# Three of four rows of each key chunk to GpSimd, and five key chunks moved from the state stage into the even projection

## The chip, the core and the metric

The kernel runs on one core of a Trainium2 chip. Its engines work side by side and meet only at semaphores: TensorE (PE) multiplies matrices, VectorE (DVE), ScalarE (ACT) and GpSimd (POOL) work on vectors, SyncE (SP) issues transfers. The metric is the device time of one execution in microseconds; lower is better. What follows reads one profiled execution of the kernel before, and the order of instructions of both.

## The reference

The reference is one step of a two-layer decoder for a prompt of 512 tokens and eight samples with one new token each. Layer 0 joins differential attention and a gated linear attention behind one input projection; layer 1 is a recurrent block; each ends with an MLP. What matters here is the attention of the eight samples to 4096 cached positions:

```python
k_past = cache_k[li, page_table].reshape(Bd, P, DA_HEADS, 2 * DA_DH)
v_past = cache_v[li, page_table].reshape(Bd, P, DA_HEADS, DA_VD)
...
def logits(qh, kp, kn):
    lp = jnp.einsum('bqhd,bkhd->bhqk', qh, kp).astype(jnp.float32) * scale + bias_p
...
a = diff_probs(logits(q1, kp1, kn1), logits(q2, kp2, kn2), lam)
out = (jnp.einsum('bhqk,bkhd->bqhd', a[..., :P], v_past.astype(jnp.float32))
       + jnp.einsum('bhqk,bkhd->bqhd', a[..., P:], v_new.astype(jnp.float32)))
```

Per cached position and head there are two dot products of length 64 (q1 with k1, q2 with k2), so a row of 512 numbers (4 heads x 2 x 64) gives eight scores.

## The kernel before

The trunk holds all 520 tokens in SBUF as 8 tiles of 128 x 520. Each weight matrix comes in chunks of 1024 x 256 into RAW; ScalarE rounds a chunk to W_hi (line 793), VectorE computes W_lo = RAW - W_hi (`split_lo`, line 1260), and TensorE forms three products per tile (line 1850). W_hi and W_lo have two slots each. The even projection has 13 chunks (the last one with one tile); behind it come 16 attention units of the prompt (four heads times four query blocks), then eight steps of the gated linear attention (the state stage), then the output projection, the MLP and layer 1.

The cache passes beside this. Keys and values of the eight samples are 64 chunks each, eight per sample; a chunk is 128 partitions x 4 rows x 512 numbers in float32, 1.05 MB, fetched by an indirect transfer that GpSimd issues (line 731) into a ring of six buffers, KV. GpSimd issues the next transfer into a buffer when both users of it are done.

A key chunk n is worked as follows. VectorE multiplies rows 0 and 1 with the sample's query, which it reads from PSUM (line 1351, `k_first`), into the first half of PROD and reduces over 64 (line 1353). GpSimd multiplies rows 2 and 3 with a copy of the query in SBUF, QB (line 664, `pool_product`), into the second half of PROD, and VectorE reduces that in line 1339 (`k_second`). Each half of PROD has one buffer: `pool_product(n)` waits for `prod1_used >= n`, that is for the reduction of product n-1. In `k_chunks` the order on VectorE is: reduction of product n-1, multiplication n, its reduction; behind the last chunk of a sample the product is reduced at once, and the sample's row maxima follow (lines 1370 to 1374).

When VectorE works key chunks is written out by hand. In the projection it is `IN_STEPS` chunks behind the split of each weight chunk from the third on, so the split for chunk c+1 stands ahead of the key chunks of iteration c. `PRE_STEPS` are two groups of three behind the projection; behind the second comes line 1529, IDENTL, with which the units start. `UNIT_STEPS` is one per unit, `GLA_STEPS` up to three per state step. The same tables set the order of transfers (`load_order`: in a unit value, key, value; in a state step pairs of key and value), the slots in which the softmax of a sample is done (`steps_by_slot`), and where GpSimd takes the inverse roots for the norms (`power`, lines 688 and 692: behind certain value chunks, or ahead of certain key chunks), on which VectorE waits in line 1525.

The value chunks are multiplied by TensorE (line 2043), two in a unit and three in a state step, behind their transfers and GpSimd's copy of the weights into PM (line 677).

## Time and profile before

| | us |
|---|---|
| median of 3 runs | 1561.07 |
| lowest and highest | 1558.76 to 1563.27 |
| profiled execution, its own time | 1562.6 |
| its span | 1560.8 |
| TensorE busy | 1409.8 (90%) |
| VectorE busy | 886.9 (57%) |
| ScalarE busy | 513.3 (33%) |
| GpSimd busy | 325.6 (21%), all but 7 of it ahead of 520 us |

Read it by stages: the projection runs to 189 us, the units start at about 222, the state stage at about 368, and its end with the output projection's start lies between 513 and 540. A busy share is the mean of a stretch; a wait in the middle of one engine's queue holds everything behind it. "Idle before" in a row is the time for which the engine stood still ahead of that group, and the arrow names what ended it.

### The profile page before, as it was taken

The numbers are of one execution on the slowest core, as the hardware profiler recorded it, in microseconds if no ns is written. First come the engines' busy times: TensorE is split into PE (matmuls) and PEld (weight loads), VectorE is DVE, ScalarE is ACT, GpSimd is POOL, SyncE is SP. The second block draws the span as 40 slices with busy tenths as digits, with TensorE's granted clock in tenths as the row PEclk, the third lists the DMA queues.
The fourth block names the chain that finished last, engine by engine and source line by source line (L and its number), as shares of the span: only waits on it lengthen the run. The fifth ranks groups of instructions, "written<-read, shape, count | busy, mean of one in ns | idle before, by whom it ended". The sixth has DMA issues, their size and how long they took to land.

```text
span 1560.8 us, 26108 instructions
## 1 busy us (share of the span) xinstructions
PE 1409.8 (90%) x11324; PEld 1269.0 (81%) x11324; DVE 886.9 (57%) x1166; ACT 513.3 (33%) x829; POOL 325.6 (21%) x263
## 2 busy tenths in 40 slices
PE   4999957798777698999999999999989999999995
PEld 3999833345334398999999999899989999999995
DVE  3398978767797526534344343788456344343534
ACT  3322254433332334212222123476343222221213
POOL 1175768766776100000000000000000000000000
PEclk8999979876677799999999999899999999999998
DMA  8477699988889721332232232222213223232221
GB/s 316 135 273 243 232 323 387 375 332 318 334 319 347 280 84 44 108 100 90 84 107 83 84 107 76 87 67 72 83 56 107 82 88 103 82 104 86 82 82 55
DMA packets 127896, 250.37 MB, mean 160 GB/s; under 512 B 5267, under 2 KB 108455, under 8 KB 111136
## 3 DMA queue, kind: packets, MB, share of 16 engines
q0 software_dynamic: 18432, 134.23, 22.5%
q1 hardware_dynamic: 104064, 106.05, 21.2%
q10 hardware_dynamic: 5288, 8.45, 1.7%
q8 instruction: 89, 1.46, 0.4%
q14 instruction: 23, 0.19, 0.0%
HBM read 241.04 MB, written 7.73 MB: 159 GB/s over the span
## 4 chain that ended last, share of the span: by engine, by line
PE 78%; DVE 9%; ACT 4%; POOL 4%; issue 2%; DMA 2%; ACTq 0%; DVEq 0%; POOLq 0%
PE PS L1850 66%; PE PS L2043 3%; POOL PROD L664 2%; DVE SC L1339 1%; DMA KV<-in_cache_v,CIDX 1%; PE PS L2127 1%; PE PS L1834 1%; PE PS L2030 1%; POOL KV L731 1%; PE PS L1842 1%; DVE ST L1571 1%; PE PS L2085 1%; DMA XSIN<-in_x_sample 1%; DVE ACC L1751 1%; PE PS L1944 1%
## 5 line engine op out<-in xcount | busy, mean ns | idle before, releaser
L1850 PE MATMUL PS<-H_hi,W_hi 128*128 128x260 f32 x1936 | 399.4, 288 | 21.2 <-DVE H_lo L1314 9.7
L1850 PE MATMUL PS<-H_lo,W_hi 128*128 128x260 f32 x1936 | 394.8, 286 | 0.0
L1850 PE MATMUL PS<-H_hi,W_lo 128*128 128x260 f32 x1936 | 394.6, 286 | 0.0
L1850 PEld LDWEIGHTS PS<-H_hi,W_hi 128*128 128x128 f32 x1936 | 304.5, 192 | 27.0 <-issue 19.2
L1850 PEld LDWEIGHTS PS<-H_lo,W_hi 128*128 128x128 f32 x1936 | 303.6, 192 | 0.0
L1850 PEld LDWEIGHTS PS<-H_hi,W_lo 128*128 128x128 f32 x1936 | 303.6, 192 | 0.0
L1260 DVE TENSOR_TENSOR W_lo<-RAW,W_hi 128x2048 fp32r<-128x2048 f32 x91 | 210.5, 2313 | 134.7 <-ACT W_hi L793 134.6
L793 ACT ACTIVATE W_hi<-RAW 128x2048 fp32r<-128x2048 f32 x91 | 173.7, 1909 | 277.2 <-PE PS L1850 276.6
L1850 PE MATMUL PS<-U_hi,W_lo 128*128 128x260 f32 x1024 | 206.4, 283 | 0.0
L1850 PE MATMUL PS<-U_lo,W_hi 128*128 128x260 f32 x1024 | 206.0, 283 | 0.0
L1850 PE MATMUL PS<-U_hi,W_hi 128*128 128x260 f32 x1024 | 206.0, 282 | 0.0
L664 POOL TENSOR_TENSOR PROD<-KV,QB 128x1024 f32<-128x1024 f32 x64 | 152.0, 2375 | 122.1 <-DVE SC L1339 93.4
L1850 PEld LDWEIGHTS PS<-U_hi,W_hi 128*128 128x128 f32 x1024 | 157.9, 188 | 0.0
L1850 PEld LDWEIGHTS PS<-U_hi,W_lo 128*128 128x128 f32 x1024 | 157.9, 188 | 0.0
L1850 PEld LDWEIGHTS PS<-U_lo,W_hi 128*128 128x128 f32 x1024 | 157.4, 188 | 0.0
L1703 DVE TENSOR_TENSOR ACC<-ACC,PS 128x520 f32<-128x520 f32 x64 | 44.5, 696 | 197.8 <-PE PS L1850 197.8
L737 POOL MEMSET ACC<- 128x4160 f32 x2 | 7.1, 3572 | 649.3 <-DVE TMP L1285 649.3
L1100 ACT ACTIVATE UF<-SQ 128x520 f32<-128x520 f32 x64 | 40.8, 638 | 253.3 <-DVE SQ L1670 253.3
L1670 DVE SCALAR_TENSOR_TENSOR SQ<-PS,RS 128x520 f32<-128x520 f32 x64 | 44.6, 699 | 109.2 <-PE PS L1850 109.2
L2043 PE MATMUL PS<-KV,PM 128*32 128x512 f32 x512 | 88.5, 780 | 19.3 <-DMA KV<-in_cache_v,CIDX 9.8
L1351 DVE TENSOR_TENSOR PROD<-KV,PS 128x1024 f32<-128x1024 f32 x64 | 77.4, 1210 | 9.0 <-ACT QB L849 8.9
L731 POOL DMA_INDIRECT KV<-in_cache_k,CIDX x64 | 70.4, 1101 | 53.2 <-DVE TMP L1285 23.1
(300 smaller groups left out, 1423.4 us busy)
## 6 DMA issues: line engine op xcount, KB each, us to landing
RAW<-in_w_up SPq DMA_DIRECT2D x32, 1024.0 KB
RAW<-in_w_down SPq DMA_DIRECT2D x32, 1024.0 KB
RAW<-in_w_in_even SPq DMA_DIRECT2D x13, 1024.0 KB
RAW<-in_w_in_odd SPq DMA_DIRECT2D x8, 1024.0 KB
RAW<-in_w_out_odd SPq DMA_DIRECT2D x5, 1024.0 KB
RAW<-in_w_out_even SPq DMA_DIRECT2D x4, 1024.0 KB
x_saved<-X ACTq DMA_DIRECT2D x1, 2080.0 KB, 9.9
X<-x_saved SPq DMA_DIRECT2D x1, 2080.0 KB, 7.7
```

Of the source, the lines that this page charges most:

```text
L664: nc.gpsimd.tensor_tensor(PROD[:, 1], KV[i % RING][:, 2:4, :], QB[:, None, b % 2, :].to_broadcast([P, 2, 512]), ALU.mult).then_inc(prod1_r ...
L731: po.indirect_dma_start(KV[i % RING].rearrange("p n f -> p (n f)"), None, cache[kind], bass.IndirectOffsetOnAxis(ap=CIDX[:, n:n + 1], axis ...
L793: A(W_hi[:, ch.slot], RAW[:, ch.slot], ACT.Copy).then_inc(w_hi_ready, 1)
L1100: A(UF[:, i], RL[:, i], ACT.Square).then_inc(uf_ready, 1)
L1260: V.tensor_tensor(W_lo[:, ch.slot], RAW[:, ch.slot], W_hi[:, ch.slot].bitcast(F32), ALU.subtract).then_inc(w_lo_ready, 1)
L1339: V.tensor_reduce(k_scores(n, 1), PROD[:, 1].rearrange("p n (j d) -> p n j d", d=DH), AX.X, ALU.add).then_inc(prod1_used, 1)
L1351: V.tensor_tensor(PROD[:, 0], KV[i % RING][:, 0:2, :], PS[:, None, 6 + b % 2, :].to_broadcast([P, 2, 512]), ALU.mult).then_inc(k_used, 1)
L1571: V.scalar_tensor_tensor(ST[:, hp, state(tb, n + 1)], ST[:, hp, state(tb, n)], DECC[:, hp, 8 * tb + n:8 * tb + n + 1], update(n, slice(0, ...
L1670: V.scalar_tensor_tensor(pair(RL[:, i]), tile_banks(ch, i), 0.0, pair(RS[:, 1]), ALU.max, ALU.mult).then_inc(banks_free[ch.par[i]], 1)
L1703: V.tensor_tensor(pair(ACC[:, m]), pair(ACC[:, m]), banks(ch.par[i]), ALU.add).then_inc(banks_free[ch.par[i]], 1)
L1850: t = MM_(PS[:, 2 * bank + j, 0:HALF], w[:, ch.slot, k, cols], x[:, k, half], start=k == 0 and n == 0, stop=k == KT - 1 and n == 2)
L2043: t = MM_(PS[32 * pos:32 * pos + 32, 4, :], PM[:, part % 2, at:at + 32], KV[i % RING][:, pos, :], start=n % 32 == 0, stop=n % 32 == 31)
```

## The change

GpSimd's product covers rows 1 to 3 of each key chunk instead of 2 and 3, and VectorE multiplies row 0 alone. PROD keeps its size of 8 KB per partition. Of VectorE's two reductions the first covers one row, the second three. The projection's iterations take 2, 2, 3, 2, 3, 2, 3, 2, 3, 2, 3 key chunks, 27 in all instead of 22. The state steps take 3, 3, 3, 2, 2, 2, 0, 0, which is 15 instead of 20. The units and the two groups ahead of them keep their numbers. The places of the roots on GpSimd follow.

```diff
-    PROD = sb("PROD", [P, 2, 2, 512], F32, r_t)
+    PROD = sb("PROD", [P, 4, 512], F32, r_t)
...
-    IN_STEPS, PRE_STEPS = 2, (3, 3)
+    IN_STEPS, PRE_STEPS = [2, 2, 3, 2, 3, 2, 3, 2, 3, 2, 3], (3, 3)
     UNIT_STEPS = [1] * 16
-    GLA_STEPS = [3, 3, 3, 3, 3, 3, 2, 0]
+    GLA_STEPS = [3, 3, 3, 2, 2, 2, 0, 0]
...
-            nc.gpsimd.tensor_tensor(PROD[:, 1], KV[i % RING][:, 2:4, :], QB[:, None, b % 2, :].to_broadcast([P, 2, 512]),
+            nc.gpsimd.tensor_tensor(PROD[:, 1:4], KV[i % RING][:, 1:4, :], QB[:, None, b % 2, :].to_broadcast([P, 3, 512]),
                                     ALU.mult).then_inc(prod1_ready, 1)
...
-        POWERS_BEFORE_K = {K_IN_UNITS: (14, 15), **{K_IN_UNITS + 3 * u + 1: (15 + u,) for u in range(1, 7)}}
-        POWER_BEHIND_V = {**{2 * u + 1: u - 1 for u in range(1, 15)}, 53: 22, 57: 23}
+        POWERS_BEFORE_K = {K_IN_UNITS: (14, 15), **{K_IN_UNITS + sum(GLA_STEPS[:u]) + 1: (15 + u,) for u in range(1, 6)}}
+        POWER_BEHIND_V = {**{2 * u + 1: u - 1 for u in range(1, 15)}, 50: 21, 53: 22, 57: 23}
...
-            pos = 4 * (n % 8) + 2 * half
-            return SC[n // 8 % SLOTS][:, :, pos:pos + 2].rearrange("p j n -> p n j")
+            pos = 4 * (n % 8)
+            rows = slice(pos + 1, pos + 4) if half else slice(pos, pos + 1)
+            return SC[n // 8 % SLOTS][:, :, rows].rearrange("p j n -> p n j")
...
-            V.tensor_reduce(k_scores(n, 1), PROD[:, 1].rearrange("p n (j d) -> p n j d", d=DH), AX.X, ALU.add).then_inc(prod1_used, 1)
+            V.tensor_reduce(k_scores(n, 1), PROD[:, 1:4].rearrange("p n (j d) -> p n j d", d=DH), AX.X, ALU.add).then_inc(prod1_used, 1)
...
-            V.tensor_tensor(PROD[:, 0], KV[i % RING][:, 0:2, :], PS[:, None, 6 + b % 2, :].to_broadcast([P, 2, 512]), ALU.mult).then_inc(k_used, 1)
+            V.tensor_tensor(PROD[:, 0:1], KV[i % RING][:, 0:1, :], PS[:, None, 6 + b % 2, :], ALU.mult).then_inc(k_used, 1)
             ve.wait_ge(k_used, n + 1)
-            link(V.tensor_reduce(k_scores(n, 0), PROD[:, 0].rearrange("p n (j d) -> p n j d", d=DH), AX.X, ALU.add))
+            link(V.tensor_reduce(k_scores(n, 0), PROD[:, 0:1].rearrange("p n (j d) -> p n j d", d=DH), AX.X, ALU.add))
...
-                k_chunks(IN_STEPS)
+                k_chunks(IN_STEPS[c - 2])
```

VectorE in the third iteration with key chunks, from the weight split (W_lo) to the next; PROD holds the products, SC a sample's scores. Before, two chunks stand between the splits:

```order
L1260 TENSOR_TENSOR W_lo<-RAW,W_hi 128x2048
L1339 TENSOR_REDUCE SC_74<-PROD 128x2x8
L1351 TENSOR_TENSOR PROD<-KV_70,PS 128x1024
L1353 TENSOR_REDUCE SC_74<-PROD 128x2x8
L1339 TENSOR_REDUCE SC_74<-PROD 128x2x8
L1351 TENSOR_TENSOR PROD<-KV_70,PS 128x1024
L1353 TENSOR_REDUCE SC_74<-PROD 128x2x8
L1260 TENSOR_TENSOR W_lo<-RAW,W_hi 128x2048
```

The same place after the change (lines behind 1262 have moved by one):

```order
L1260 TENSOR_TENSOR W_lo<-RAW,W_hi 128x2048
L1340 TENSOR_REDUCE SC_74<-PROD 128x3x8
L1352 TENSOR_TENSOR PROD<-KV_70,PS 128x512
L1354 TENSOR_REDUCE SC_74<-PROD 128x8
L1340 TENSOR_REDUCE SC_74<-PROD 128x3x8
L1352 TENSOR_TENSOR PROD<-KV_70,PS 128x512
L1354 TENSOR_REDUCE SC_74<-PROD 128x8
L1340 TENSOR_REDUCE SC_74<-PROD 128x3x8
L1352 TENSOR_TENSOR PROD<-KV_69,PS 128x512
L1354 TENSOR_REDUCE SC_74<-PROD 128x8
L1260 TENSOR_TENSOR W_lo<-RAW,W_hi 128x2048
```

Three chunks stand there now, each with a short multiplication and a long reduction; the last row of each chunk is still followed directly by the split.

GpSimd in the fifth state step (DMA rows are issues of transfers, NRT and NRS the two operations of a root). Before:

```order
L664 TENSOR_TENSOR PROD<-KV_70,QB 128x1024
L731 DMA KV_69<-in_cache_v,CIDX 128x2048
L731 DMA KV_70<-in_cache_k,CIDX 128x2048
L688 TENSOR_SCALAR NRT<-NSQ 128x2
L692 TENSOR_TENSOR NRS<-NRT,EPSC 128x2
L664 TENSOR_TENSOR PROD<-KV_69,QB 128x1024
L731 DMA KV_70<-in_cache_v,CIDX 128x2048
L731 DMA KV_69<-in_cache_k,CIDX 128x2048
L664 TENSOR_TENSOR PROD<-KV_69,QB 128x1024
L731 DMA KV_69<-in_cache_v,CIDX 128x2048
L731 DMA KV_69<-in_cache_k,CIDX 128x2048
```

After:

```order
L664 TENSOR_TENSOR PROD<-KV_69,QB 128x1536
L731 DMA KV_69<-in_cache_k,CIDX 128x2048
L731 DMA KV_69<-in_cache_v,CIDX 128x2048
L688 TENSOR_SCALAR NRT<-NSQ 128x2
L692 TENSOR_TENSOR NRS<-NRT,EPSC 128x2
L664 TENSOR_TENSOR PROD<-KV_70,QB 128x1536
L731 DMA KV_69<-in_cache_k,CIDX 128x2048
L731 DMA KV_70<-in_cache_v,CIDX 128x2048 x2
```

The step holds two products and five issues there instead of three and six; the root still stands ahead of its second product.

## Rows read from the trace of the kernel before

**Rows 1.** The page's chain that ended last, shares by engine.
```profile
PE 78%; DVE 9%; ACT 4%; POOL 4%; issue 2%; DMA 2%; ACTq 0%; DVEq 0%; POOLq 0%
```

**Rows 2.** Windows by stage: busy us (instructions) by engine, PEclk, DMA share, GB/s.
```profile
75.00:189.00 114.00, 113.47 (x923) 111.00 (x922) 102.56 (x85) 31.32 (x34) 77.81 (x42) 1.00 0.69 240
189.00:222.00 33.00, 18.08 (x89) 12.79 (x89) 25.94 (x33) 17.42 (x26) 23.10 (x14) 0.73 0.89 312
222.00:368.00 146.00, 118.23 (x676) 61.52 (x676) 106.22 (x162) 62.28 (x208) 107.76 (x107) 0.83 0.92 353
368.00:513.00 145.00, 110.85 (x832) 56.33 (x831) 118.83 (x210) 48.62 (x164) 98.58 (x84) 0.69 0.90 338
```

**Rows 3.** GpSimd's product: the page's group (busy, mean ns | idle), and its wait.
```profile
L664 POOL TENSOR_TENSOR PROD<-KV,QB 128x1024 f32<-128x1024 f32 x64 | 152.0, 2375 | 122.1 <-DVE SC L1339 93.4
...
POOL PROD L664 <- DVE SC L1339: 93.4, 53, 6.9
```

**Rows 4.** VectorE's timeline in the projection: start, us, engine, line, operation.
```profile
83.36 1.21 DVE L1339 TENSOR_REDUCE SC<-PROD 128x16 f32<-128x1024 f32 x1
...
87.24 1.22 DVE L1339 TENSOR_REDUCE SC<-PROD 128x16 f32<-128x1024 f32 x1 [0.29 <-POOL PROD L664]
...
90.88 2.29 DVE L1260 TENSOR_TENSOR W_lo<-RAW,W_hi 128x2048 fp32r<-128x2048 f32 x1
93.09 1.22 DVE L1339 TENSOR_REDUCE SC<-PROD 128x16 f32<-128x1024 f32 x1
```

**Rows 5.** GpSimd's timeline there.
```profile
75.00 2.42 POOL L664 TENSOR_TENSOR PROD<-KV,QB 128x1024 f32<-128x1024 f32 x1 [28.52 <-ACT QB L849]
...
84.73 2.41 POOL L664 TENSOR_TENSOR PROD<-KV,QB 128x1024 f32<-128x1024 f32 x1 [0.41 <-DVE SC L1339]
...
88.61 2.40 POOL L664 TENSOR_TENSOR PROD<-KV,QB 128x1024 f32<-128x1024 f32 x1 [0.36 <-DVE SC L1339]
```

**Rows 6.** VectorE's timeline at the first units: operations of 512 elements.
```profile
224.90 0.67 DVE L1507 TENSOR_TENSOR PR<-PS,BIAS 128x512 f32<-128x512 f32 x1
225.60 0.69 DVE L1510 TENSOR_REDUCE MX<-PR 128x2 f32<-128x512 f32 x1
```

**Rows 7.** GpSimd's and VectorE's timelines where they overlap.
```profile
112.27 2.40 POOL L664 TENSOR_TENSOR PROD<-KV,QB 128x1024 f32<-128x1024 f32 x1 [0.36 <-DVE SC L1339]
...
112.33 2.38 DVE L1373 TENSOR_TENSOR SC<-SC,SBL 32x32 f32<-32x32 f32 x1
...
160.39 2.40 POOL L664 TENSOR_TENSOR PROD<-KV,QB 128x1024 f32<-128x1024 f32 x1 [0.37 <-DVE SC L1339]
...
160.81 4.12 DVE L1260 TENSOR_TENSOR W_lo<-RAW,W_hi 128x2048 fp32r<-128x2048 f32 x1
164.86 1.21 DVE L1351 TENSOR_TENSOR PROD<-KV,PS 128x1024 f32<-128x1024 f32 x1
...
260.10 1.07 DVE L1525 SCALAR_TENSOR_TENSOR NRS<-NSQ,NRS 128x1 f32<-128x1 f32 x1
```

**Rows 8.** VectorE's timeline: the operation with which the units start.
```profile
221.48 0.27 DVE L1529 TENSOR_SCALAR IDENTL<-CONST,LAM 128x128 f32<-128x128 f32 x1
```

**Rows 9.** One turn in the units, VectorE's and GpSimd's timelines.
```profile
275.61 1.22 DVE L1339 TENSOR_REDUCE SC<-PROD 128x16 f32<-128x1024 f32 x1
...
282.07 0.56 POOL L692 TENSOR_TENSOR NRS<-NRT,EPSC 128x1 f32<-128x1 f32 x1
...
282.92 1.21 DVE L1339 TENSOR_REDUCE SC<-PROD 128x16 f32<-128x1024 f32 x1
```

**Rows 10.** VectorE's timeline: the last operation of state steps 1, 6, 7 and 8.
```profile
387.39 0.42 DVE L1519 TENSOR_SCALAR OTC<-PS 128x256 f32<-128x256 f32 x1
...
484.13 0.42 DVE L1519 TENSOR_SCALAR OTC<-PS 128x256 f32<-128x256 f32 x1 [1.12 <-ACT OT L1020]
...
499.90 0.42 DVE L1519 TENSOR_SCALAR OTC<-PS 128x256 f32<-128x256 f32 x1
...
512.88 0.42 DVE L1519 TENSOR_SCALAR OTC<-PS 128x256 f32<-128x256 f32 x1 [2.80 <-ACT OT L1020]
```

More of the change, by code:

```diff
@@ L489, in take @@
                 k, v = k + (kind == "k"), v + (kind == "v")
-        take("k" * (IN_STEPS * 11 + sum(PRE_STEPS)))
+        take("k" * (sum(IN_STEPS) + sum(PRE_STEPS)))
         for n in UNIT_STEPS:
@@ L507, in steps_by_slot @@
     def steps_by_slot():
-        done = [IN_STEPS * (i + 1) for i in range(11)]
+        done = [sum(IN_STEPS[:i + 1]) for i in range(11)]
         for n in (*PRE_STEPS, *UNIT_STEPS):
@@ L678, in weights @@
                                   SC[b % SLOTS][:, :, 16 * half:16 * half + 16].rearrange("p j n -> p n j")).then_inc(pm_ready, 1)
-        K_IN_UNITS = sum(UNIT_STEPS) + 2 * 11 + sum(PRE_STEPS)
-        POWERS_BEFORE_K = {K_IN_UNITS: (14, 15), **{K_IN_UNITS + 3 * u + 1: (15 + u,) for u in range(1, 7)}}
-        POWER_BEHIND_V = {**{2 * u + 1: u - 1 for u in range(1, 15)}, 53: 22, 57: 23}
+        K_IN_UNITS = sum(UNIT_STEPS) + sum(IN_STEPS) + sum(PRE_STEPS)
+        POWERS_BEFORE_K = {K_IN_UNITS: (14, 15), **{K_IN_UNITS + sum(GLA_STEPS[:u]) + 1: (15 + u,) for u in range(1, 6)}}
+        POWER_BEHIND_V = {**{2 * u + 1: u - 1 for u in range(1, 15)}, 50: 21, 53: 22, 57: 23}
         def power(u):
```

## The prediction

> **What bounds the kernel now.** The chain that ended last gives TensorE 78% [rows 1], but that is a mean over unlike stages, so the stage table comes next [rows 2]. In the even projection (75 to 189 us) TensorE is busy 113.47 of 114 us at a granted clock of 1.00. From 189 us on it is not: 18 of 33 us before the units, 118 of 146 in the attention units, 111 of 145 in the state stage, at a granted clock of 0.69 to 0.83, while VectorE is busy 73 to 82% and the transfers 0.89 to 0.92 of the time. Behind 540 us the change touches nothing. So two questions decide: does the projection still hide its key chunks, and what do the other stages wait for? GpSimd's product of a chunk takes 2375 ns, 64 times, and GpSimd waits 93.4 us in all, at 53 of them, for VectorE's reduction in line 1339 [rows 3].
>
> That wait is a round trip. The half of PROD that GpSimd writes has one buffer: product n+1 may start only when VectorE has reduced product n, and VectorE reduces in its own order. Read two turns in the projection: reduction starts at 83.36, product starts 1.37 us later at 84.73 and takes 2.41, the next reduction starts at 87.24 [rows 4, 5]. A turn is 3.88 us. Where VectorE also splits a weight chunk (90.88, 2.29 us), the turn is 93.09 - 87.24 = 5.85 us. Two chunks and one split are 9.7 us of the roughly 11.7 that TensorE needs for a weight chunk (some 11.5 us of products; the projection's 114 us hold 9.7 chunks), so today the round trip hides, just.
>
> **The turn after the change.** VectorE's multiplication and its own reduction shrink to 512 elements: 0.67 and 0.69 us [rows 6] where 1024 take 1.2. Its second reduction grows from 1024 to 1536: 0.53 us more, about 1.75. VectorE's work per chunk falls from 3.65 to 3.1 us, 64 x 0.55 = 35 us of busy time. But that is not what a turn is made of. A turn is reduction (1.75), 0.15 to GpSimd, product, 0.1 back. No row has a GpSimd product of 1536 elements. From below, if 0.4 us of the 2375 ns were fixed, it is 1975 x 1.5 + 400 = 3.36 us; from above it is proportional, 3.6. I take 3.5, since an operation of this size is nearly all elements. The turn is 5.5 us instead of 3.88, and VectorE idles 2.4 us in each.
>
> [...]
>
> **The weight split and the product exclude each other.** In three rows VectorE took far longer than its work. The 32x32 addition in line 1373 took 2.38 us once, from 112.33 to 114.71; GpSimd's product ran from 112.27 to 114.67 [rows 7]. The split at 160.81 took 4.12 us instead of 2.29; a product ran from 160.39 to 162.79, and the split ended 2.14 us behind it [rows 7]. The inverse norm in line 1525, one number per partition, took 1.07 us at 260.10 [rows 7]. All three read two SBUF tensors. VectorE's key multiplication, which has one input in PSUM, runs beside products at its normal 1.2 us. So a VectorE instruction with two SBUF inputs waits for a GpSimd product in progress. Before the change this is rare: the split is issued 3.64 us behind the reduction, when the product has just ended. Afterwards VectorE reaches the split 1.66 + 1.42 = 3.1 us behind the reduction, and the product runs from 1.9 to 5.4. Each split meets it. The turn with a split is 5.4 + 2.07 (164.86 less 162.79) = 7.5 us; without exclusion it would be 5.5.
>
> The Trainium skill, SBUF, State Buffer, section "SBUF: two separate sides", states this as an exclusive lock that the first to start holds for the whole instruction. By that rule a faster VectorE in front of a longer product is hurt, as here; were the rule wrong, the rival below without exclusion would hold.
>
> **Term A, projection and the six chunks behind it.** 27 + 6 = 33 chunks are reduced until the units start, 28 before. The first product still starts at 75.00 [rows 5], so the first reduction at 78.6. From there to the 32nd reduction are 31 turns, nine of them with a split: 9 x 7.5 + 22 x 5.5 = 188.5, which ends at 267.1. VectorE's part of the last chunk, the row maxima, whose addition again waits for the product, and three such waits earlier add about 8: the identity scaling in line 1529, which opens the units, comes at about 275 instead of 221.48 [rows 8]. **+53 us.** Nothing makes this good: TensorE waits for W_lo about 30 us in the projection (its last chunk starts near 213), ScalarE waits for TensorE, and the ring of six buffers is full. The five chunks move out of the later stages at 5.5 us each, and the other 28 pay 1.6 each. Bounds: product 3.36 gives +48, 3.6 gives +56; without exclusion 31 x 5.5 makes +32.
>
> **Term B, the 16 attention units**, one key chunk each as before. Here the turn passes through more of GpSimd's queue: reduction 275.61, product, the issues of a value and a key chunk, the root (NRS at 282.07, 0.56), which VectorE awaits before the next reduction at 282.92 [rows 9]. That is 7.31 us, and becomes 7.31 + 1.13 (product) + 0.53 (reduction) = 9.0. The stage is 146/16 = 9.1 us a unit [rows 2], with transfers 0.92 busy, so some units wait for something else and hide it. Bounds: 0 (all hidden) and 16 x 1.66 = 27. I take **+15**, near the middle, because units as short as 7.31 exist but the mean stands at the new floor.
>
> **Term C, the state stage.** Five steps with three key chunks took (484.13 - 387.39)/5 = 19.35 us, one with two 15.8, one with none 13.0 [rows 10]. Now three have three, three have two, two have none. With three the products add 3.4 us to GpSimd's side of the cycle and VectorE's side saves 1.6; between -1.6 and +3.4 I take +1 each, +3. With two: 15.8 + 0.6 = 16.4, three times -3. The seventh falls from 15.8 to 13.0. **-9 us.** Bounds: +2, if the long product also sets the pace with two; -15, if transfers did: five chunks of 1.05 MB at 353 GB/s [rows 2] are 2.97 us each.
>
> **Sum.** 53 + 15 - 9 = +59. Against the profiled execution (1562.6 us; span 1560.8) 1621.6; the median of the runs is 1.5 lower: **1620 us**.
>
> **Rivals.**
> 1. No exclusion (18%). The two slow instructions had another cause. A is +32, B +12, C -9: 1596 us. For it: most splits took 2.29. Against it: both long rows end with, or one clean duration behind, a product, to within 0.2 us.
> 2. The pause lets transfers catch up (10%). Units and state stage move 0.92 and 0.90 of the time; if transfers alone set their pace, the longer product costs nothing there and five chunks less give -15, with a fuller ring a little more: A +53, B 0, C -18, 1596 us. Against it: the root and the product appear in the cycle of [rows 9] without a transfer.
> 3. The other side (5%): VectorE's order, not the round trip, sets the pace. Then the 0.55 us per chunk is a gain and the five chunks save 15: about 1545 us. It decides at one number. A must fall to the 8 us or so that B and C give back: 31 turns, nine of them 2 us longer, would have to fit in about 145 us, 4.1 us a turn, so the product in 2.1 us. Three rows would have to be faster than two rows are now.
> 4. TensorE's clock (4%). Waits of 5 to 7 us in the projection may lower it, as in the later stages (0.69 to 0.83 [rows 2]). If it stayed at 1.2 GHz, the last seven chunks would take 23 instead of 11.7 us and VectorE would wait for W_hi: about 1670 us. A short fall costs nothing, since TensorE then has room.
>
> **Chances.** Forecast 60%, rivals 18, 10, 5 and 4%, no change that can be told 3% (a measurement of this kernel tells about 0.3%, 5 us). Slower by more than that 92%, same 3%, faster 5%. The range goes from A at its low product with rival 1 or 2 and a good state stage (1586) to A high, B 25, C +2 with the median's offset (1644).
>
> **What would show it.** Product 3.5 us; reductions of the product 5.5 us apart; W_lo splits of about 4.5 us that end 2.1 us behind a product; TensorE idle before every third chunk's products; projection's products ending near 219 us instead of 188.5, line 1529 (now 1530) near 275; VectorE's busy time lower by only 5 to 15 us, since the waiting splits count as busy. Units near 10 us, two-chunk steps near 16. It is wrong if the product takes under 3.2 us, if reductions stand closer than 5.2 us, or if the units catch up what the projection lost.

## The result: 94 us slower

The kernel after the change takes 1654.96 us, the median of 4 runs (1653.11 to 1657.72), against 1560.76 (1558.76 to 1563.27) for the kernel before on the same chip: a ratio of 1.0604, 95% interval 1.0583 to 1.0626. The forecast was 1620 with a range up to 1644. The direction was right, the size 35 us short.

Two windows of the kernel after, projection and the stretch behind it, then units and state stage (columns as in [rows 2]), answer to [rows 2]:

```profile
77.60:223.70 146.10, 123.49 (x923) 118.65 (x922) 105.60 (x90) 30.60 (x33) 111.04 (x45) 0.91 0.58 202
223.70:292.50 68.80, 22.89 (x89) 15.47 (x89) 41.30 (x46) 18.18 (x27) 43.77 (x21) 0.60 0.65 215
292.50:455.00 162.50, 119.74 (x662) 62.41 (x663) 111.85 (x158) 59.74 (x196) 124.37 (x105) 0.82 0.84 311
455.00:610.00 155.00, 114.01 (x866) 57.55 (x864) 95.42 (x199) 52.64 (x180) 103.31 (x82) 0.72 0.81 294
```

TensorE no longer fills the projection (123.49 of 146.10 us), and transfers run at 202 GB/s there instead of 240. Behind it the transfers, 0.92 busy in the units before, are at 0.84: something slower than they are sets the pace. The page's chain and groups and the view of the waits (us in all, times, longest) of the kernel after name it; they answer to [rows 1, 3]:

```profile
PE 65%; DVE 14%; POOL 11%; ACT 4%; issue 3%; DMA 2%; ACTq 0%; DVEq 0%; POOLq 0%
...
L664 POOL TENSOR_TENSOR PROD<-KV,QB 128x1536 f32<-128x1536 f32 x64 | 221.0, 3453 | 125.2 <-DVE SC L1340 96.2 <-ACT QB L849 28.9
L1340 DVE TENSOR_REDUCE SC<-PROD 128x24 f32<-128x1536 f32 x64 | 112.0, 1750 | 62.8 <-POOL PROD L664 62.6
```
```profile
POOL PROD L664 <- DVE SC L1340: 96.2, 54, 8.7
DVE SC L1340 <- POOL PROD L664: 62.6, 29, 2.8
```

GpSimd waits as long for VectorE's reduction as before (96.2 against 93.4 us), although its products take 69 us more, and VectorE now waits 62.6 us for products, 5.4 before. The two engines stand still by turns: that is the round trip. VectorE's timeline at its first turns (start, us, engine, line, operation) answers to [rows 4], GpSimd's to [rows 5]:

```profile
81.25 1.76 DVE L1340 TENSOR_REDUCE SC<-PROD 128x24 f32<-128x1536 f32 x1 [2.33 <-POOL PROD L664]
82.92 0.68 DVE L1352 TENSOR_TENSOR PROD<-KV,PS 128x512 f32<-128x512 f32 x1
83.63 0.69 DVE L1354 TENSOR_REDUCE SC<-PROD 128x8 f32<-128x512 f32 x1
84.36 4.44 DVE L1260 TENSOR_TENSOR W_lo<-RAW,W_hi 128x2048 fp32r<-128x2048 f32 x1
88.72 1.74 DVE L1340 TENSOR_REDUCE SC<-PROD 128x24 f32<-128x1536 f32 x1
...
94.23 1.76 DVE L1340 TENSOR_REDUCE SC<-PROD 128x24 f32<-128x1536 f32 x1 [2.46 <-POOL PROD L664]
```
```profile
83.15 3.49 POOL L664 TENSOR_TENSOR PROD<-KV,QB 128x1536 f32<-128x1536 f32 x1 [2.00 <-DVE SC L1340]
86.80 2.87 POOL L731 DMA_INDIRECT KV<-in_cache_k,CIDX  x1 [0.15 <-issue]
```

A turn with a split is 88.72 - 81.25 = 7.47 us, one without 94.23 - 88.72 = 5.51. The product ends at 86.64 and the split at 88.80, 2.16 behind it.

**Where the 95 us of the span came from**, by five points that every trace has: ScalarE's copy of the tile LR out of PSUM (end of the projection), IDENTL (the units open), VectorE's first operation on the samples' state (line 1487, 1486 before; the units end), the last clamp of the state stage (OTC, line 1520, 1519 before), and H_lo behind it, with which the output projection's input is split. Start us of each:

| | LR | units open | units end | last clamp | first H_lo | span |
|---|---|---|---|---|---|---|
| before | 188.5 | 221.5 | 365.3 | 512.9 | 521.4 | 1560.8 |
| after | 223.7 | 292.5 | 456.1 | 605.0 | 618.7 | 1655.9 |
| e1, rows alone | 215.7 | 258.0 | 416.2 | 587.4 | 597.1 | 1635.8 |
| e2, steps alone | 196.8 | 249.9 | 392.0 | 531.4 | 542.4 | 1581.9 |
| e3, split with one SBUF input | 214.8 | 283.5 | 446.3 | 596.4 | 609.5 | 1649.4 |
| e10, three rows in state stage | 190.0 | 222.9 | 360.1 | 528.8 | 537.5 | 1576.1 |
| e12, two buffers | 208.5 | 257.3 | 408.6 | 550.1 | 563.0 | 1601.1 |
| e14, five ahead of SN | 188.6 | 215.9 | 364.9 | 513.1 | 521.9 | 1560.7 |
| e17, steps untangled | 196.8 | 236.6 | 382.3 | 520.6 | 533.8 | 1571.5 |
| e18, after untangled | 222.2 | 278.3 | 440.8 | 590.2 | 603.1 | 1640.5 |

After against before: +71.0 until the units open, +19.8 in the units (163.6 against 143.8), +1.3 in the state stage, +5.2 from there to H_lo, -2.2 in all that follows. The start scatters: the first product, 75.00 before, came at 77.63 after.

TensorE took 10 us longer for the projection's 923 products (123.49 against 113.47), at a granted clock of 0.91 instead of 1.00. The turns without a split show nothing of it: they keep 5.4 to 5.5 us throughout.

### The profile page after: what moved, and what is told of

Same layout as the page of the kernel before. It is cut to its first block, busy times and chain, and to the rows that moved or that the text cites. A ratio compares the mean times of both kernels' runs of the same rounds, so it can differ in the third digit from the quotient of the medians.

```text
span 1655.9 us, 26110 instructions
## 1 busy us (share of the span) xinstructions
PE 1427.2 (86%) x11324; PEld 1280.3 (77%) x11324; DVE 887.0 (54%) x1166; ACT 513.3 (31%) x829; POOL 396.2 (24%) x263
## 4 chain that ended last, share of the span: by engine, by line
PE 65%; DVE 14%; POOL 11%; ACT 4%; issue 3%; DMA 2%; ACTq 0%; DVEq 0%; POOLq 0%
PE PS L1851 57%; POOL PROD L664 8%; DVE SC L1340 5%; DVE W_lo L1260 2%; POOL KV L731 2%; PE PS L2044 1%; PE PS L1835 1%; DMA out_gla_prompt<-ST 1%; PE PS L1945 1%; ACT W_hi L793 1%; DVE SC L1354 1%; DMA XSIN<-in_x_sample 1%; DVE PROD L1352 1%; PE PS L1843 1%; DVE TMP L1285 1%
## 5 line engine op out<-in xcount | busy, mean ns | idle before, releaser
L1260 DVE TENSOR_TENSOR W_lo<-RAW,W_hi 128x2048 fp32r<-128x2048 f32 x91 | 214.9, 2362 | 130.9 <-ACT W_hi L793 130.8
L664 POOL TENSOR_TENSOR PROD<-KV,QB 128x1536 f32<-128x1536 f32 x64 | 221.0, 3453 | 125.2 <-DVE SC L1340 96.2
L1340 DVE TENSOR_REDUCE SC<-PROD 128x24 f32<-128x1536 f32 x64 | 112.0, 1750 | 62.8 <-POOL PROD L664 62.6
```

Source lines behind the costliest of these rows:

```text
L664: nc.gpsimd.tensor_tensor(PROD[:, 1:4], KV[i % RING][:, 1:4, :], QB[:, None, b % 2, :].to_broadcast([P, 3, 512]), ALU.mult).then_inc(prod1 ...
L1260: V.tensor_tensor(W_lo[:, ch.slot], RAW[:, ch.slot], W_hi[:, ch.slot].bitcast(F32), ALU.subtract).then_inc(w_lo_ready, 1)
L1340: V.tensor_reduce(k_scores(n, 1), PROD[:, 1:4].rearrange("p n (j d) -> p n j d", d=DH), AX.X, ALU.add).then_inc(prod1_used, 1)
```

## The two halves of the change apart

**e1** takes the kernel after and gives it the old steps. **e2** takes the new steps and the old rows.

```diff
 e1, against after
-    IN_STEPS, PRE_STEPS = [2, 2, 3, 2, 3, 2, 3, 2, 3, 2, 3], (3, 3)
+    IN_STEPS, PRE_STEPS = [2] * 11, (3, 3)
...
-    GLA_STEPS = [3, 3, 3, 2, 2, 2, 0, 0]
+    GLA_STEPS = [3, 3, 3, 3, 3, 3, 2, 0]
...
 e2, against after
...
-            nc.gpsimd.tensor_tensor(PROD[:, 1:4], KV[i % RING][:, 1:4, :], QB[:, None, b % 2, :].to_broadcast([P, 3, 512]),
+            nc.gpsimd.tensor_tensor(PROD[:, 1], KV[i % RING][:, 2:4, :], QB[:, None, b % 2, :].to_broadcast([P, 2, 512]),
...
```

> GpSimd multiplies three rows and VectorE one, but the projection takes in 22 key chunks and the state stage 17, as in the kernel before. Theory (the reduction-product-reduction turn, longer by the product, sets the pace): turns of 5.5 us, 7.5 with a weight split; from the first reduction near 78.6 us 26 turns, nine with a split, are 9 x 7.5 + 17 x 5.5 = 161 us, so the units open near 250 us instead of 221.5 (+29); the units take 20 us more, as after the change; five state steps with three chunks take 3 us more each (+15). In all about 1625 us (1610 to 1640). Rival (the five moved chunks do the harm, the split of rows little): under 1590 us, units opening before 235 us.

Measured: 1634.94 us, ratio 1.0455 (1.0416 to 1.0493), +71 us.

> Two rows for GpSimd and two for VectorE as before, but 27 key chunks in the projection and twelve in the state stage. Theory (the round trip of 3.88 us is still short enough): three chunks and a split are 5.85 + 2 x 3.88 = 13.6 us beside 11.7 of TensorE, two are 9.7, so on average the projection still just hides them; its end moves by 0 to 8 us, the state stage gives back 9 to 15. In all 1548 to 1565 us, GpSimd's product at 2.38 us. Rival (the moved chunks do the harm: transposes and the low-rank product behind the row maxima): 1590 us or more, the units opening at 250 us or later.

Measured: 1585.10 us, ratio 1.0154 (1.0116 to 1.0192), +24 us by the ratio (18 to 30; the medians differ by 21). Within these intervals the two add up to the 94 of the change. (The expectations miscount the state stage's key chunks: it has 20 with the old steps and 15 with the new.) e1's time lies in the theory's range; its units opened 8 us later than said (258.0 against 250), took 14 us more where 20 stood, and the state stage took 23.6 more where 15 stood. e2 fell between theory and rival, and nearer to the rival: 20 us above the theory's range and 5 below the rival's 1590, with the units opening at 249.9 where the rival said 250. Two things were open: what e2's 28 us before the units are, and whether the turn is what costs in e1.

## Is it the round trip, and is it the exclusion?

**e12** gives GpSimd's product two buffers and leaves its length.

```diff
-    PROD = sb("PROD", [P, 4, 512], F32, r_t)
+    PROD = sb("PROD", [P, 1, 512], F32, r_t)
+    PROD2 = sb("PROD2", [P, 2, 3, 512], BF16, r_t + 2048)
...
-                po.wait_ge(prod1_used, n)
+                po.wait_ge(prod1_used, n - 1)
...
```

> The kernel after, with two buffers for GpSimd's product. To make room the product is written as bfloat16, so that the past scores are rounded; the number of elements is the same. Theory (the turn of 5.5 us is the single buffer's round trip): GpSimd starts a product while VectorE still reduces the one ahead, reductions 4.3 to 4.9 us apart instead of 5.5, the projection ends 10 to 20 us earlier than 223.7, the units open at 255 to 275 us instead of 292.5, in all 1605 to 1635 us. Rival (GpSimd's and VectorE's exclusion and GpSimd's own work set the pace, whatever the buffers): over 1645 us.

Measured: 1598.65 us, ratio 1.0244 (1.0209 to 1.0279), 56 us less than after, 6 us better than the theory's best end. The group of e12:

```profile
L666 POOL TENSOR_TENSOR PROD<-KV,QB 128x1536 bf16<-128x1536 f32 x64 | 223.1, 3487 | 39.1 <-ACT QB L851 28.7 <-DVE SC L1342 9.4
L1342 DVE TENSOR_REDUCE SC<-PROD 128x24 f32<-128x1536 bf16 x64 | 111.9, 1748 | 14.5 <-POOL PROD L666 13.8
```

Product and reduction take what they took (3487 and 1748 ns), so the narrower type changed nothing but the room; GpSimd's wait for the reduction fell from 96.2 to 9.4 us and VectorE's for the product from 62.6 to 13.8. The longer product costs mainly because it stands in a round trip with one buffer: shown, for 56 of the 94 us.

**e3** takes the exclusion out of the projection's weight splits by giving them one operand from PSUM, a constant. W_lo is then not the true remainder; the number of elements is the same.

```diff
-            V.tensor_tensor(W_lo[:, ch.slot], RAW[:, ch.slot], W_hi[:, ch.slot].bitcast(F32), ALU.subtract)
+            V.tensor_tensor(W_lo[:, ch.slot], RAW[:, ch.slot], PS[:, 4, None, 0:256].to_broadcast([P, KT, 256]), ALU.mult)
```

> The kernel after, but in the projection the weight split reads one SBUF operand and one PSUM operand (W_lo = RAW x 2^-12 from a constant in PSUM, so W_lo is not the true remainder there; same number of elements). Theory (a VectorE instruction with two SBUF inputs and a GpSimd product exclude each other): the splits take 2.3 us instead of 4.45, the turn with a split 5.5 to 5.9 instead of 7.5, nine of them, and the projection ends 16 to 22 us earlier; 1630 to 1640 us. Rival (the splits are slow for another reason, or the time is not on the path): splits of 4.4 us, or faster splits and an unchanged 1655 us.

Measured: 1653.00 us, ratio 1.0588 (1.0551 to 1.0626), within 2 us of after. In its trace the units open 9.0 us earlier, 2.2 of which are an earlier first reduction (79.01 against 81.25). VectorE's and GpSimd's timelines of e3, the same turn:

```profile
79.01 1.75 DVE L1343 TENSOR_REDUCE SC<-PROD 128x24 f32<-128x1536 f32 x1 [2.31 <-POOL PROD L664]
...
82.11 2.29 DVE L1261 TENSOR_TENSOR W_lo<-RAW,PS 128x2048 fp32r<-128x2048 f32 x1
84.46 1.75 DVE L1343 TENSOR_REDUCE SC<-PROD 128x24 f32<-128x1536 f32 x1
```
```profile
80.91 3.51 POOL L664 TENSOR_TENSOR PROD<-KV,QB 128x1536 f32<-128x1536 f32 x1 [2.00 <-DVE SC L1343]
84.58 0.99 POOL L731 DMA_INDIRECT KV<-in_cache_k,CIDX  x1 [0.15 <-issue]
```

The exclusion is real: beside the same product the split takes 2.29 us instead of 4.44 and the turn 5.45 instead of 7.47. The price that was put on it in the splits, 16 to 22 us, was wrong: only three of the nine turns with a split became short, the others kept 7.5 to 8.2 us. In the kernel after only three splits (84.36, 97.33, 115.80) are long at all. VectorE's timeline of after shows what makes the others:

```profile
130.99 0.19 DVE L1374 TENSOR_TENSOR SC<-SC,SBL 32x32 f32<-32x32 f32 x1
131.21 0.42 DVE L1375 TENSOR_REDUCE ROWMX<-SC 128x8 f32<-128x256 f32 x1
131.55 2.28 DVE L1260 TENSOR_TENSOR W_lo<-RAW,W_hi 128x2048 fp32r<-128x2048 f32 x1
...
148.15 1.95 DVE L1381 TENSOR_SCALAR MDIAG<-CONST,M 8x8 f32<-8x8 f32 x1
150.02 2.27 DVE L1260 TENSOR_TENSOR W_lo<-RAW,W_hi 128x2048 fp32r<-128x2048 f32 x1
...
160.82 0.42 DVE L1386 TENSOR_TENSOR SC<-SC,PS 128x256 f32<-128x256 f32 x1
163.53 2.29 DVE L1260 TENSOR_TENSOR W_lo<-RAW,W_hi 128x2048 fp32r<-128x2048 f32 x1 [2.29 <-ACT W_hi L793]
```

Work of the samples' softmax stands ahead of the split. In four of the six turns it is a small instruction of it that waits out the product (MDIAG, 64 numbers, 1.95 us): the same exclusion, only not in the split. In the two others the split waits 2.29 us for W_hi, because ScalarE's exponentials, which wait for VectorE's line 1386, stand ahead of W_hi in its queue. By then the product is over. What the exclusion costs in all instructions together no run tells, since e3 takes it out of the splits alone.

**e7** gives the kernel before two buffers (VectorE multiplies in place in the ring, and the ring is released behind its first reduction).

```diff
-                po.wait_ge(prod1_used, n)
+                po.wait_ge(prod1_used, n - 1)
...
-            V.tensor_tensor(PROD[:, 0], KV[i % RING][:, 0:2, :], PS[:, None, 6 + b % 2, :].to_broadcast([P, 2, 512]), ALU.mult).then_inc(k_used, 1)
+            V.tensor_tensor(KV[i % RING][:, 0:2, :], KV[i % RING][:, 0:2, :], PS[:, None, 6 + b % 2, :].to_broadcast([P, 2, 512]), ALU.mult).then_inc(k_used, 1)
...
-                po.wait_ge(k_used, n + 1)
+                po.wait_ge(k_used, 2 * n + 2)
```

> The kernel before (two rows each, old steps), with two buffers for GpSimd's product: VectorE multiplies in place in the ring, and the ring's buffer is released behind VectorE's first reduction. Theory (the single buffer makes the round trip, and the round trip is what the units and the stretch ahead of them wait for): GpSimd's wait for the reduction falls from 93 us to under 40, the units take 5 to 16 us less; 1540 to 1556 us. Rival (transfers or VectorE's own order set the pace there): within 5 us of the kernel before.

Measured: 1563.90 us, ratio 1.0011 (0.9994 to 1.0027): no change. GpSimd's wait for the product's reduction fell, but its release of the ring took a new one (waits of e7):

```profile
POOL KV L731 <- DVE SC L1353: 75.1, 30, 5.4
...
POOL PROD L664 <- DVE SC L1339: 28.1, 11, 6.7
```

So this run doesn't tell whether the round trip sets the pace with two rows: it was partly replaced by another. The stages of e14, below, look at it from the other side.

## Where a longer product costs

**e9** and **e10** give GpSimd three rows in one part of the kernel before only; **e8** gives it one row everywhere, **e11** one row in the units.

```diff
+    def own(n):
+        return 4 - (3 if n < 28 else 2)                # e9
+        return 4 - (3 if n >= 44 else 2)               # e10
+        return 4 - (1 if 28 <= n < 44 else 2)          # e11
...
-            nc.gpsimd.tensor_tensor(PROD[:, 1], KV[i % RING][:, 2:4, :], QB[:, None, b % 2, :].to_broadcast([P, 2, 512]),
+            nc.gpsimd.tensor_tensor(PROD[:, own(n):4], KV[i % RING][:, own(n):4, :], QB[:, None, b % 2, :].to_broadcast([P, 4 - own(n), 512]),
...
```

> The kernel before with its old steps, but GpSimd multiplies three rows of the 28 key chunks ahead of the units and two of all others. Theory (the longer turn costs in each stage what e1_split_only showed there, and nothing is given back later): the units open near 257 us, +35 against before, units and state stage as before: about 1597 us (1590 to 1603). Rival (the ring and the transfers catch up part of it in the units): under 1588 us.

Measured: 1596.82 us, ratio 1.0225 (1.0185 to 1.0265). The units open at 257.2 and take 144.7: nothing is caught up.

> The kernel before, GpSimd multiplies three rows only of the 20 key chunks behind chunk 43, seventeen in the state stage and three in the last units. The prediction's term: a state step with three chunks 1 us longer (VectorE's saving against the longer product), in all +5 us, 1562 to 1568. The rival, from e1_split_only: the round trip, product and reduction, sets the pace here too, 1.08 + 0.53 us for each chunk, three in a step, 4.4 to 4.8 us a step; in all +20 to +25 us, about 1584.

Measured: 1578.93 us, ratio 1.0133 (1.0101 to 1.0165). (All twenty of these chunks lie in the state stage.) The stage takes 168.7 us instead of 147.6, +21.1, about 1.1 us for each chunk, two thirds of the 1.08 + 0.53 of the rival.

> The opposite split: GpSimd multiplies one row of each key chunk and VectorE three, old steps. Theory (what counts is the round trip and which engine waits): product about 1.25 us, VectorE's own work 4.2 us per chunk and so longer than the round trip of 2.2 us; VectorE's busy time up 35 us, two chunks and a split 10.7 us, still beside TensorE's 11.7; the ten chunks ahead of the units cost 0.3 to 0.5 us each more, the units within 5 us: 1560 to 1580 us. Rival (time follows GpSimd's total product time, 71 us more gave +71 us, so 71 us less should give some of it back): under 1545 us.

Measured: 1558.13 us, ratio 0.9974 (0.9959 to 0.9990). Product 1281 ns, VectorE's busy time +30 us.

> The kernel before, GpSimd multiplies one row only of the 16 key chunks of the units (28 to 43) and two elsewhere. Theory (in the units the turn of reduction, product and root is part of what is waited for; in e8_gpsimd_one_row they took 136.5 instead of 143.8 us): units 7 us shorter, everything else as before, 1553 to 1557 us. Rival (e8's gain came from the state of the ring when the units opened, later and fuller): within 2 us of before.

Measured: 1556.01 us, ratio 0.9969 (0.9948 to 0.9990). The units take 136.4 us in e8 and 138.0 in e11, but 137.2 in e10 too, where their code is that of before (143.8), and 149.0 in e14: such a difference lies within what the stage scatters by. What remains is the 0.3% of the timed runs, at the edge of what can be told. The time is not proportional to GpSimd's work: 69 us more cost 71, 70 us less give 4.

**e14** puts five instead of three chunks ahead of the wait at SN (VectorE's addition in line 1437, which needs TensorE's last result ahead of the units), **e15** moves two chunks from the stretch into the projection.

```diff
-    IN_STEPS, PRE_STEPS = 2, (3, 3)
+    IN_STEPS, PRE_STEPS = [2] * 11, (5, 1)                             # e14
+    IN_STEPS, PRE_STEPS = [2, 2, 2, 3, 2, 2, 2, 3, 2, 2, 2], (3, 1)    # e15
```

> The kernel before, of the six key chunks between projection and units five instead of three ahead of VectorE's wait for TensorE at SN. Theory (this stretch is VectorE's own chunks, 3.84 us each, plus a wait of 5.71 us at 209.52): SN comes near 211.5 us with little or no wait, the units open 4 to 6 us earlier, near 216.5 us; 1553 to 1558 us. Rival (TensorE's rotations and the bias behind them, not VectorE, hold the units): TensorE waits as much longer, within 2 us of before.

Measured: 1561.06 us, ratio 0.9986 (0.9961 to 1.0011).

> Two rows each; 24 key chunks in the projection and four (three ahead of SN, one behind it) instead of six between it and the units; all else as before, state stage too. Theory (room for 24 in the projection, stretch at 3.84 us a chunk): projection 0 to 3 us longer, stretch 7 to 8 us shorter, 1552 to 1558 us. Rival (no room, or a later wait takes it up): within 2 us of before or slower.

Measured: 1564.53 us, ratio 1.0021 (0.9997 to 1.0046). e15 missed its theory: the units opened at 219.9, only 1.6 us earlier. e14's stretch did what the theory said, the units opened at 215.9 (216.5 expected), and it was worth nothing: they ended at 364.9, as before. Windows of e14, units and state stage:

```profile
215.90:364.90 149.00, 118.12 (x669) 60.82 (x669) 105.43 (x159) 64.26 (x203) 106.04 (x102) 0.82 0.91 341
364.90:513.10 148.20, 115.04 (x840) 58.69 (x838) 119.56 (x216) 51.05 (x173) 100.92 (x89) 0.68 0.90 335
```

Neither theory nor rival had this. The reading that fits is that with two rows the transfers set the pace behind the opening: 48 loads in the units and 52 in the state stage, 100 in 291.4 us before, 2.91 us each, 2.97 in e14, and 95 loads at 2.96 in e2 and 2.99 in e17, whenever the units opened. No run made the transfers shorter, so this is argued and not shown. After the change 95 loads take 312.5 us, 3.29 each, and 3.28 in e18: there the turn is longer than the transfers.

## What the moved chunks cost

Here "the stretch" is what lies between the projection's end and the units: six key chunks on VectorE, and on TensorE and ScalarE the low-rank product of the gates, the transposes and the bias. SN stands behind VectorE's first three chunks. **e5** places three buffers 32 bytes higher, so that LR lies over the scores of a later sample and VectorE's wait for the low-rank product (`la_done`) stands ahead of chunk 32 instead of 24; **e4** is the same edit in the kernel after. **e6** puts TensorE's slot 11 behind the twelve transposes. **e13** moves two chunks instead of five.

```diff
-    LR = sb("LR", [P, T], F32, r_t + 14336 - TB)
+    LR = sb("LR", [P, T], F32, r_t + 14368 - TB)       # e4, e5; QTOK and QB 32 bytes up too
...
-                if b == 3:
+                if b == 4:
                     ve.wait_ge(la_done, 2)
 e13, against before
-    IN_STEPS, PRE_STEPS = 2, (3, 3)
+    IN_STEPS, PRE_STEPS = [2, 2, 2, 3, 2, 2, 2, 3, 2, 2, 2], (3, 3)
-    GLA_STEPS = [3, 3, 3, 3, 3, 3, 2, 0]
+    GLA_STEPS = [3, 3, 3, 3, 2, 2, 2, 0]
...
```

> The kernel after, with three buffers placed 32 bytes higher, so that the low-rank tile overlaps the score tiles of samples 4 and 5 only, and VectorE's wait for the low-rank product stands ahead of chunk 32 instead of chunk 24. Theory (that wait inside the projection costs 6 us on the path, with TensorE waiting for VectorE in return): VectorE is not held at 234 us, the units open 5 to 9 us earlier, 1646 to 1650 us. Rival (VectorE would wait for the same thing a moment later): within 2 us of the kernel after, 1653 to 1657.

Measured: 1651.86 us, ratio 1.0577 (1.0540 to 1.0614). The units open at 285.9, 6.6 us earlier, as the theory said; the time is 3 less, which the intervals don't separate from nothing.

> Two rows each and the new steps, as in e2_steps_only, with the three buffers 32 bytes higher, so VectorE's wait for the low-rank product stands ahead of chunk 32 and not of chunk 24, which is inside the projection. Theory: in e2 VectorE was held 5.60 us ahead of chunk 24, and the row maxima that TensorE awaits ahead of its transposes came that much later; without the wait the units open 5 to 9 us earlier than the 249.9 us of e2, in all 1574 to 1579 us. Rival (VectorE's chunks are only pushed about, what counts is that TensorE waits behind three more chunks): within 3 us of 1585.

Measured: 1581.93 us, ratio 1.0129 (1.0083 to 1.0175). The units open at 244.3 (249.9 in e2), as the theory said; the time, 3 less than e2's, is not the theory's and can't be told from e2's.

> As e2_steps_only, with TensorE's part of slot 11 (the maxima of sample 2, which wait for VectorE's row maxima) behind the twelve transposes instead of ahead of them. Theory: the 12 transposes started at about 217 us in e2 because they stood behind that wait; now they start near 207 us, SN comes 8 to 12 us earlier than 237.35, and the units open 6 to 12 us earlier: 1572 to 1579 us. Rival (the chunks on VectorE's side set the end of the stretch, not the transposes): SN's wait shrinks but VectorE meets it at the same time, within 3 us of 1585.

Measured: 1586.24 us, ratio 1.0161 (1.0122 to 1.0201): nothing, with the units opening at 252.1.

> Two rows each; the projection takes in 24 key chunks (22 before, 27 after the change) and the state stage 18 (three each in four steps, two in three). Theory (VectorE has room for about 24 chunks in the projection; what is above that stands serial behind it, at 3.84 us each, and that is the 28 us by which e2's units opened late): the units open at 221 to 228 us, the state stage gives back 3 to 5 us; 1555 to 1566 us. Rival (a moved chunk costs by the order in which the engines wait for each other, e2's 24 us being five such chunks): two chunks cost 8 to 10 us, 1568 us or more.

Measured: 1573.98 us, ratio 1.0074 (1.0046 to 1.0102), the rival's number: two moved chunks cost 12 us with 24 chunks in the projection, so lack of room is not all of it. e6's timeline shows where its gain went: the chain moved to the next engine.

```profile
231.39 0.42 ACT L854 ACTIVATE SC<-SC 128x256 f32<-128x256 f32 x1 [12.91 <-DVE SC L1385]
...
239.61 0.32 DVE L1437 TENSOR_TENSOR SN<-PS,TB 128x32 f32<-128x32 f32 x2 [8.19 <-PE PS L1998]
```

From 24 chunks on, sample 2 is complete inside the projection, and its softmax steps, which each engine has at fixed slots, fall into the stretch behind it. There they stand ahead of TensorE's transposes (slot 11 waits for MDIAG) and of ScalarE's bias (slot 11 waits for VectorE), and VectorE waits for both at SN. **e17** takes all three waits apart, with the steps alone; **e18** in the kernel after.

```diff
 e5's edit, and on TensorE
             t.then_inc(la_done, 1)
-        slot(11)
         for i in range(12):
...
+        slot(11)
         pe.wait_ge(tr_copied, 12)
 on ScalarE
-        slot(11)
         act.wait_ge(sample_in, 1)
...
             A(BIAS[:, 2 * i:2 * i + 2], PS[:, 3:5, :], ACT.Copy).then_inc(bias_ready, 1)
+        slot(11)
         slot(12)
```

> Two rows each and the new steps, with all three couplings in the stretch behind the projection taken apart: the three buffers 32 bytes higher (as in e5), TensorE's part of slot 11 behind the twelve transposes (as in e6), and ScalarE's part of slot 11 (the exponentials of sample 2, which wait for VectorE) behind the evictions of the bias instead of ahead of them. Theory (in e5 and e6 the chain only moved on to the next engine: in e6 ScalarE waited 12.91 us for VectorE ahead of the bias, and VectorE then 8.19 us for SN): the wait at SN falls from 8 us to under 1.5, the units open at 234 to 238 us instead of 244.3 (e5) and 252.1 (e6); 1568 to 1575 us. Rival (VectorE's nine chunks at 3.84 us each set the stretch by themselves): no more than 2 us better than e5, 1579 us or more.

Measured: 1572.52 us, ratio 1.0062 (1.0038 to 1.0086); the units open at 236.6, both as the theory said.

> The kernel after (three rows and one) with the same three edits as e17_steps_untangled. Theory: VectorE is held neither at 234.3 us (5.99) nor at SN (6.66), so the units open 11 to 14 us earlier than 292.5 us, at 278 to 282 us; 1641 to 1647 us, the rest of the loss being the longer turn. Rival (the long product hides these waits, GpSimd being late anyway): as e4_la_late, 1650 us or more.

Measured: 1642.10 us, ratio 1.0509 (1.0477 to 1.0540), 13 us less than after; the units open at 278.3 instead of 292.5, again as the theory said. SN in e2, in e17, in after and in e18 (VectorE's timelines):

```profile
237.35 0.31 DVE L1437 TENSOR_TENSOR SN<-PS,TB 128x32 f32<-128x32 f32 x2 [8.05 <-PE PS L1998]
```
```profile
224.14 0.31 DVE L1437 TENSOR_TENSOR SN<-PS,TB 128x32 f32<-128x32 f32 x2 [0.59 <-DVE TB L1434]
```
```profile
240.30 0.69 DVE L1352 TENSOR_TENSOR PROD<-KV,PS 128x512 f32<-128x512 f32 x1 [5.99 <-PE PS L1972]
...
275.65 0.31 DVE L1438 TENSOR_TENSOR SN<-PS,TB 128x32 f32<-128x32 f32 x2 [6.66 <-PE PS L1999]
```
```profile
261.46 0.31 DVE L1438 TENSOR_TENSOR SN<-PS,TB 128x32 f32<-128x32 f32 x2
```

With the steps alone, the first edit by itself brought the opening forward by 5.5 us and the time by 3, which is within the noise, and the second brought nothing (the third wasn't tried by itself); together they bring the opening forward by 13.2 us and the time by 13. The order couplings are worth 13 us in e2's 24 and 13 in the change's 94: shown for the three together.

**e16** tests the sixth state step of the kernel after, where VectorE waits 4.90 us for the root.

```diff
-        POWERS_BEFORE_K = {K_IN_UNITS: (14, 15), **{K_IN_UNITS + sum(GLA_STEPS[:u]) + 1: (15 + u,) for u in range(1, 6)}}
+        POWERS_BEFORE_K = {K_IN_UNITS: (14, 15), **{K_IN_UNITS + sum(GLA_STEPS[:u]) + (u < 5): (15 + u,) for u in range(1, 6)}}
```

> The kernel after, with the root of state step 5 ahead of GpSimd's product of chunk 62 instead of behind it and four load issues. Theory (in that step, 22.6 us long with two chunks, VectorE waits 4.90 us at 567.66 for the root behind the long product): the step falls to 17 to 19 us, in all 3 to 5 us less than after, 1650 to 1652 us. Rival (the weights PM behind the same product hold TensorE, whatever the root does): the step keeps 21 us or more, within 2 us of 1655.

Measured: 1656.68 us, ratio 1.0595 (1.0552 to 1.0637). The step takes 21.1 us instead of 22.6, but the one ahead of it 15.8 instead of 14.1, and the whole stage 148.6 against 148.9: the rival.

No version here beats the kernel before by more than the 0.3% of e8 and e11.

## Why the prediction was right in kind and short in size

**The turn: right.** Product 3.453 us (3.5 said), turns 5.5 and 7.5, splits ending 2.16 behind the product. From the first reduction at 81.25 to the 24th at 228.47 the nine turns with a split are 7.4 to 8.4 us long and the fourteen others 5.4 to 5.5. e12 shows that it is the round trip.

**Nine splits that meet the product: wrong in cause, near in sum.** Three did. In four of the other turns a small instruction ahead of the split met it, and in two ScalarE's queue held W_hi; each cost 2 to 3 us. The nine turns took 70.5 us, 67.5 said. That the sum came near is luck as far as these two go.

**VectorE's busy time 5 to 15 us lower: wrong.** It is 887.0 us, as before (886.9). The halved operations save 34 us; the same 34 come back as waiting inside instructions: 4.4 in the splits, 7.9 in MDIAG, 4.3 in line 1374, the rest in single instructions of the gate preparation. The exclusion reaches further than the splits.

**Term A, +53, measured +71: the step that failed is "22 x 5.5", the turns without a split.** It has no term for waits on other engines in the stretch behind the projection. Two of the 22 turns, the 24th and the 29th (reductions at 228.47 and 263.64), took 13.28 and 12.22 us, 14.5 more than said: in the one VectorE waited 5.99 us for the low-rank product, in the other 6.66 for SN. In e18 they took 7.20 and 5.59. The rest of the 18 us is 2.6 of later start and 3.0 in the turns with a split, less 2.2 behind the 32nd reduction (5.8 us, 8 said) and 0.5 in the other turns. The waits were to be read in the kernel before: `la_done` is awaited ahead of chunk 24, which the change moves into the projection, and the softmax of sample 2 moves ahead of the transposes. e18's units open 14.2 us earlier than after's, 1.2 of it by an earlier first reduction (80.08 against 81.25) and 13.0 by order alone. Without these waits and the later start term A would be 55. The end of the projection, 219 said, came at 223.7.

The prediction's other count of the same term, five chunks at 5.5 us and 28 at 1.6, makes 72 and not 53; it stood there without a word on what hides the rest, and that it lies near 71 is luck, since it has no term for these waits either.

**Term B, +15, measured +19.8:** within its bounds; the turn is mis-sized by little. With the code of before the unit stage scatters between 137.2 us (e10) and 149.0 (e14); with three rows and the new steps it is steady, 162.5 to 163.6 in after, e3 and e18.

**Term C, -9, measured +1.3: the step that failed is its sign for VectorE's side.** The prediction let VectorE's saving (1.6) offset the product in steps with three chunks. In a round trip the longer reduction adds, up to 1.08 + 0.53 us a chunk. e10 measured +21.1 for twenty chunks, against the 5 that the prediction's rule gave. The steps alone gave back 8.2 of the 9 (e2: 139.4 us), the rows took it.

**No term for what lies behind the last clamp:** +5.2. There the 64 KB transfer out_gla_prompt takes 11.0 us instead of 5.3 and ScalarE's H_hi waits 7.1 us for it; e2, e12 and e18 have that wait too (4.9 to 6.7 us, and 11.0 to 12.9 between clamp and H_lo, 8.5 before). It goes with the new steps; why wasn't tried.

**Rivals.** No exclusion: wrong, e3, though its price in the splits was less than said. Transfers catch up: wrong, e9 and the 0.84. TensorE at 1.2 GHz throughout: wrong, 0.91 in the projection. Faster: the product took 3.45 us, not 2.1.

The sum in hindsight: A 55 + 13 + 3, B 20, C 1, tail 5, rest -2 is the 95 of the span.

## What to carry to other kernels

Read a table of steps as an order on every engine: moving work across a point moves each wait that hangs on its count, and taking away one of several such waits only shows the next (3 us, within the noise, and 0 for two of them singly, 13 for the three). A shared buffer's round trip has both engines' parts in it; work taken from one engine to spare it is no gain if the other then holds the buffer. And the stages whose transfers were 0.9 busy neither gained from an earlier opening (e14) nor hid a turn that had become longer than their transfers.

## What the runs showed of the hardware

The exclusion hits small instructions too. MDIAG (8x8, one SBUF tensor and a scalar operand from SBUF, line 1381) took 1.95 us at 148.15 and 1.2 on the mean, 0.22 before. The Trainium skill, SBUF — State Buffer, section "SBUF: two separate sides", has the lock for a VectorE operation in a 2-port mode or with two SBUF inputs. The split with one SBUF input in e3 (2.29 us beside a product) agrees with it; MDIAG would have to run in a 2-port mode, which no run here shows.

It works the other way round as well: GpSimd's issue of an indirect load mostly takes 0.98 us, but 2.87 at 86.80, while VectorE's split ran until 88.80. A split of the kernel after started at 150.02 and one of e3, with one SBUF input, at 141.89; GpSimd's issue came 0.2 us behind each:

```profile
150.22 2.93 POOL L731 DMA_INDIRECT KV<-in_cache_k,CIDX  x1
```
```profile
141.89 2.27 DVE L1261 TENSOR_TENSOR W_lo<-RAW,PS 128x2048 fp32r<-128x2048 f32 x1
142.09 0.98 POOL L731 DMA_INDIRECT KV<-in_cache_k,CIDX  x1
```

In the kernel after it took 2.93 us and ended 0.86 behind the split; in e3 it took 0.98 with the split running. The same section of the Trainium skill tells that a VectorE operation in a 2-port mode keeps GpSimd from writing the descriptors of a transfer. The split is not of that kind but has two SBUF inputs, and these rows show it doing the same.
